# The U pass of the expert layers, written half by half and then chunk by chunk

## What is computed

```python
def peer_ffn(x, w_q, sub_keys, u_tab, v_tab):
    ...
    def block(xb):
        q = (xb @ w_q).reshape(blk, PEER_HEADS, 2, PEER_HALF)
        ...
        idx = ...                      # the 16 best of 128 x 128 experts, for 8 heads
        g = jax.nn.softmax(top_s, axis=-1)
        u = u_tab[idx]
        v = v_tab[idx]
        act = jax.nn.gelu(jnp.einsum('thkd,td->thk', u, xb).astype(jnp.float32), approximate=False)
        return jnp.einsum('thk,thkd->td', (g * act).astype(xb.dtype), v)
```

## Time and profile before

| | |
|---|---|
| runs | 4380.94, 4379.13, 4376.19 us; median 4379.13 us |
| the profiled execution | 4380.36 us, of which 4378.6 us lie between its first and its last instruction (the span) |
| TensorE matmuls | busy 4121.6 us (94% of the span), 27,209 records |
| DVE / ACT | busy 2531.3 us (58%) / 1181.0 us (27%) |
| mean granted TensorE clock | 0.967 of full speed |

### The profile page before, as it was taken

The page is one execution under the profiler, slowest core; times in us unless marked ns, Lnnn a source line. Parts: engine busy times, 40 slices in busy tenths (PEclk is TensorE's granted clock), DMA queues, the critical chain, the costliest instruction groups (busy, mean ns, idle before and its releaser), DMA issues. The chain is left out here.

```text
span 4378.6 us, 74431 instructions
## 1 busy us (share of the span) xinstructions
PE 4121.6 (94%) x27209; PEld 3707.9 (85%) x27209; DVE 2531.3 (58%) x4688; ACT 1181.0 (27%) x1587; POOL 38.3 (1%) x43
## 2 busy tenths in 40 slices
PE   8777779999999999999998988999999999999997
PEld 8754479999999998888887567999999998888886
DVE  3642247777776535555554755777777534555555
ACT  2101042233333321111113443333333332111112
POOL 0000000000000010000000000000000001000000
PEclk9869789999999999999999988999999999999999
DMA  3026523334444565555541012233454466555562
GB/s 108 24 77 208 185 77 105 111 129 173 155 170 169 178 236 197 187 197 189 198 146 67 29 39 96 102 124 135 167 185 154 166 207 221 198 187 199 184 201 82
DMA packets 321924, 652.36 MB, mean 149 GB/s; under 512 B 26241, under 2 KB 157442, under 8 KB 321154
## 3 DMA queue, kind: packets, MB, share of 16 engines
q1 hardware_dynamic: 318978, 642.36, 43.1%
q0 software_dynamic: 2816, 8.40, 0.5%
HBM read 509.00 MB, written 141.53 MB: 149 GB/s over the span
## 5 line engine op out<-in xcount | busy, mean ns | idle before, releaser
L1797 DVE TENSOR_TENSOR experts_ul<-experts_u,experts_uh 128x1024 fp32r<-128x1024 f32 x512 | 627.1, 1225 | 1068.5 <-ACT experts_uh L1691 1062.2
L1584 PE MATMUL ps<-peer_x_then_r_xh,experts_ul 128*128 128x260 f32 x4096 | 1166.4, 285 | 0.0
L1585 PE MATMUL ps<-experts_over_x_xl,experts_uh 128*128 128x260 f32 x4096 | 1154.9, 282 | 0.0
L1586 PE MATMUL ps<-peer_x_then_r_xh,experts_uh 128*128 128x260 f32 x4096 | 1153.6, 282 | 0.0
L1691 ACT ACTIVATE experts_uh<-experts_u 128x1024 fp32r<-128x1024 f32 x512 | 540.6, 1056 | 1094.6 <-PE ps L1648 1085.2
L1646 PE MATMUL ps<-experts_over_a_ah,experts_ul 128*128 128x512 f32 x2048 | 796.9, 389 | 0.0
L1648 PE MATMUL ps<-experts_over_a_ah,experts_uh 128*128 128x512 f32 x2048 | 796.9, 389 | 0.0
L1647 PE MATMUL ps<-experts_over_a_al,experts_uh 128*128 128x512 f32 x2048 | 796.8, 389 | 0.0
L1584 PEld LDWEIGHTS ps<-peer_x_then_r_xh,experts_ul 128*128 128x128 f32 x4096 | 771.7, 188 | 0.0
L1586 PEld LDWEIGHTS ps<-peer_x_then_r_xh,experts_uh 128*128 128x128 f32 x4096 | 770.1, 188 | 0.0
L1585 PEld LDWEIGHTS ps<-experts_over_x_xl,experts_uh 128*128 128x128 f32 x4096 | 769.8, 188 | 0.0
(11 more groups left out here) (347 smaller groups left out, 4681.7 us busy)
## 6 DMA issues: line engine op xcount, KB each, us to landing
experts_u<-peer_u SPq DMA_DIRECT2D x256, 512.0 KB, 3.3
experts_u<-peer_v SPq DMA_DIRECT2D x256, 512.0 KB, 3.3
hidden<-experts_act SPq DMA_DIRECT2D x256, 260.0 KB, 2.2
gates<-experts_over_b_g SPq DMA_DIRECT2D x128, 512.0 KB, 3.0
experts_over_b_g<-gates SPq DMA_DIRECT2D x128, 512.0 KB, 4.9
experts_act<-hidden SPq DMA_DIRECT2D x256, 256.0 KB, 3.6
mla_ct<-cache SPq DMA_DIRECT2D x64, 320.0 KB, 3.8
pa_ct<-cache SPq DMA_DIRECT2D x64, 320.0 KB, 3.7
```

Of the source, the lines that this page charges most:

```text
L1584: pe.matmul(o, ul[:, b % 4, c], xh[:, c, h, 0:TH], start=(c == 0), stop=False)
L1585: pe.matmul(o, uh[:, b % 4, c], xl[:, c, h, 0:TH], start=False, stop=False)
L1586: mm = pe.matmul(o, uh[:, b % 4, c], xh[:, c, h, 0:TH], start=False, stop=(c == KC - 1))
L1797: v.tensor_tensor(ul[:, b % 4], u[:, b % 2], uh[:, b % 4].bitcast(F32), ALU.subtract).then_inc(split_done, 1)
```

## The change

The loops over halves and chunks change places, and each of the three products gets a loop over the halves of its own. For one chunk TensorE now issues the low-weight matmul for half 0 and half 1, the high-weight one by `xl` for both halves, and the high-weight one by `xh` for both halves. Both halves' sums are open from the first two matmuls of a block to its last two. The matmuls of a block, their operands, the order of the additions within each sum, the waits ahead of the block and the signal at its end stay.

```diff
                     pe.wait_ge(split_done, n + 1)
                     pe.wait_ge(gelu_ready, n + 1)
-                    for h in range(2):
-                        o = hidden_of[b % 2][:, h]
-                        for c in range(KC):
-                            pe.matmul(o, ul[:, b % 4, c], xh[:, c, h, 0:TH], start=(c == 0), stop=False)
-                            pe.matmul(o, uh[:, b % 4, c], xl[:, c, h, 0:TH], start=False, stop=False)
-                            mm = pe.matmul(o, uh[:, b % 4, c], xh[:, c, h, 0:TH], start=False, stop=(c == KC - 1))
+                    o = hidden_of[b % 2]
+                    for c in range(KC):
+                        for h in range(2):
+                            pe.matmul(o[:, h], ul[:, b % 4, c], xh[:, c, h, 0:TH], start=(c == 0), stop=False)
+                        for h in range(2):
+                            pe.matmul(o[:, h], uh[:, b % 4, c], xl[:, c, h, 0:TH], start=False, stop=False)
+                        for h in range(2):
+                            mm = pe.matmul(o[:, h], uh[:, b % 4, c], xh[:, c, h, 0:TH], start=False, stop=(c == KC - 1))
                     mm.then_inc(block_done, 1)
```

## The result

| | before | changed |
|---|---|---|
| runs | 11, 4376.19 to 4383.48 us | 11, 4383.31 to 4392.36 us |
| median | 4379.13 us | 4390.28 us |
| profiled execution, its span | 4380.36 us, 4378.6 us | 4387.58 us, 4385.8 us |

What follows compares the result with a forecast made beforehand. The prediction took TensorE's stream of matmuls in the U passes as the bound. Its terms added 0 + 0 + 0 to the profiled 4380.36 us, forecast as the median 4379.1 us, range 4367 to 4391 us.

Steps and rivals of the forecast that it cites:

- What bounds the kernel: In the two U passes, 957 us each and 44% of the span, TensorE's stream of matmuls sets the time.
- The 118.95 ns: Distance between matmul starts where only U blocks run, from 765 matmuls in 91 us; 10.6 ns beyond the 108.3 for columns.
- What the change leaves: Matmuls, loads (12,288 each), waits, signal, other engines' instructions and transfers stay as they were, costed at nothing.
- (a) Repeats: In a U block, 32 of 48 matmuls repeat the stationary operand instead of 16, 4,096 more in all; saving 0.
- (b) Changes of bank: In U blocks, 47 bank changes instead of 1, 11,776 more in all; cost 0, at most 11.8 us up or down.
- slower rival: U passes: a toll at each change of bank and half; 4391 us at 1 ns each, at most 4497 us; chance 0.04.
- (c) The second matmul behind a wait: At about 170 block starts behind other work, the second matmul's 0.08 us delay could go, at most 14 us; taken as 0.
- faster rival: U blocks: a repeat into another bank is cheap, giving 4292 or 4336 us, or 4365 us from block starts; chance 0.04.
- The rule beside the trace: Skill page's gap, 110.8 ns for 260 columns without a load between; 66 us off, 4313 us; the trace does not agree.
- sign of being wrong: The prediction is wrong if matmul distance depends on repeats and banks together in a way neither shows alone.
- The sum: Whole kernel: 4380.36 us profiled plus 0 + 0 + 0; forecast at the median of the runs, 4379.1 us.
- no difference: Whole kernel's time stays within about 0.2%, 8.8 us, 4370.4 to 4387.9 us; chance 0.92.

## Why the prediction was wrong

**What bounds the kernel** held: TensorE's stream, no wait ahead of a U block, and a longer distance between matmuls arrived in the time almost one for one. The 118.95 ns are a little low: the count of 765 takes in records that only reach into the window, and from starts 15 blocks apart it is 119.3 ns, so that 11.0 and not 10.6 ns were beyond the 108.3. Nothing hangs on it.

**What the change leaves** held as far as it was listed: the matmuls and loads, their lengths, the waits, the V pass, the other engines. What the list left out is what failed. A matmul's distance was taken to be the same wherever its operands lie. It hangs on how the address of the moving operand in flight lies to that of the weights loaded meanwhile, and on how this relation moves from matmul to matmul; that succession is what the new order changes.

**(a) Repeats** of the operand: the price of zero is borne out. Where the relation rests, a matmul takes 120.0 ns with 16 repeats in a block and 120.0 ns with 32; and with 32 a block takes 5,707 or 5,760 ns, by the spacing alone.

**(b) Changes of bank**: the price of zero is borne out, and better than the rows could: without any change within the block it is still 5,760.0 ns. But the text set this term's bound as the bound of the whole step from one matmul to the next. That the bound, 11.8 us or 4391 us, nearly met the measured 4390.28 us is no merit: the slower rival's mechanism, a toll at banks, was shown wrong. Its other half, "alternating moving operands", was near the cause, but what costs is not the alternation; at 1,152 bytes apart the alternating order is the faster one.

**(c) The second matmul behind a wait** stayed late (203 ns behind the first in both kernels, the median of 170 such blocks), so zero was right there too. The **faster rival** did not come.

**The step that failed** is the argument in (b) by rows of other places, and with it the zero that it gave to the step from one matmul to the next: it measured 0.7 ns for each of 12,288 matmuls. Line 698 and the V pass have their own addresses, so they could show that banks cost nothing, and could not show that this order at these addresses costs nothing. The trace of before held the warning: with one order and one set of matmuls, half 0 took 2,859 ns and half 1 2,867 ns of a block, and within half 0 a steady chunk took 356.7 ns for three matmuls, in half 1's last chunks 359 to 361. In the earlier trace rows that drowns in steps of 10 ns; the prediction saw "0.12 and 0.13" and called them alike. Averages over whole halves would have shown a distance that depends on which operand is read. Multiplied by 12,288 matmuls, the 0.7 ns that can't be seen in two starts are 8.5 of the 9.4 us that the U passes lost. The prediction's sign of being wrong, a distance that depends on repeats and banks together, was not it either: neither of them counts.

**The rule beside the trace** was rightly set aside: no run had a mean step near 110.8 ns, and each repeat has a load of its own as before.

**The sum and the chances.** The time lay in the range, but no difference had 0.92 and slower 0.04. The range had been made for an unknown of 1 ns at 11,776 places; the chances should have been made from it as well, since the edge of "no difference" lay at 0.75 ns.

**What stays open.** No run shows why a relation is cheap. All block times are whole multiples of 6.67 ns (856 to 865 of them), and no run says what that step is. Theory E gave the right numbers for the block at 1,280 bytes and with the weights 128 higher, and for the V pass at minus 128 and minus 256. It doesn't say why going between 64 and 192 is cheap and between 0 and 128 is not, why the changed order at 1,088 bytes, where the relation goes through 64, 0, 192 and 128, averages 120.0 ns (steps of 115 ns are among them, and longer ones make up for them), nor why the V pass, whose relation stands still at 0, is at its best there.

## What to carry to other kernels

Where TensorE is the bound, a reordering of matmuls is not neutral even if every operand and every load stays: it changes in what order the relations of two addresses follow each other, that of the moving operand and that of the weights loaded meanwhile. This was worth up to 1% of a U block (5,706.7 to 5,766.7 ns) and 3% of a V matmul (226.7 to 233.3 ns). So give such operands fixed, deliberate offsets, and look at the distance of matmuls averaged over blocks and by operand before and after, not at single starts. And an edit of an allocation list that only moves small tiles can cost 1% of the kernel, in a stage that it doesn't mention.

## What the runs showed of the hardware

- 64 bytes in the address of the weights are worth 6.7 ns of 226.7 in a matmul of 512 columns, some 41 us of this kernel, although each load (188 ns in its record with either address) is over 35 ns or more before the next matmul starts. The Trainium skill, page "TensorE: Matmul & The Clock Gate", section "What happens when you issue a matmul", says: "Loading the next tile's weights doesn't steal SBUF read bandwidth from the running matmul." The measurement doesn't agree, as far as two reads that never met couldn't care how their addresses lie: the two kernels with the weights 64 bytes higher differ only in the addresses of the V pass's moving operands, and the V pass goes from 233.3 to 226.7 ns. No run shows which of the two reads waits.
- The cost repeats with 256 bytes of the relation in the V pass: 226.7 ns at 0 and at minus 256, 232.4 at plus and minus 128, 233.3 at plus 32 and plus 64, 228.9 at minus 64. In the U pass the distance is 118.9 ns where the relation goes between 64 and 192, and 120.0 ns where it rests at 64 or at 192 or goes between 0 and 128.
- Alternating between two PSUM banks with both sums open costs nothing that a block of 48 matmuls shows: 5,760.0 ns with 47 changes and with none. A matmul with the operand of the one before gains nothing either: 120.0 ns with 16 and with 32 of them in a block, at a resting relation.
- A block's time on TensorE repeats to within 0.1 ns a matmul, in both layers and from run to run, so that a profile settles differences that 11 runs of the whole kernel don't.
